# Grouped-query attention by single heads in another order, a convolution beside the projections, and a delta rule on four quadrants

## What is computed

```python
def odd_mixer(h, l, P, rope, ctx):
    z = jnp.dot(h, P['w_in_cd'][li])
    qkv, gate, beta_logit, decay_logit, qg, kg, vg = split_last(z, ...)
    y_c, delta_state = gated_delta_mixer(qkv, gate, ...)      # conv of 4 taps, silu, delta rule
    q = rms_norm(qg...); k = rms_norm(kg...)                   # 8 query heads, 2 key heads, width 64
    ...                                                        # rope; sample: 128 cached keys in front
    o = sweep_query_blocks(lambda qb: gqa_block(qb, k, v), q)  # softmax(q k) v
    return jnp.dot(concatenate([y_c, o]), P['w_out'][l])

def chunk_gated_delta_rule(q, k, v, beta, g, s0):              # chunks of 64 rows, forward and backward
    decay = jnp.exp(where(incl, G[..., :, None] - G[..., None, :], -inf))
    a = jnp.where(strict, einsum('nbhid,nbhjd->nbhij', kb, k) * decay, 0.0)
    sol = triangular_solve(a + eye(C), [kb * exp(G), v * beta])  # w, u
    ...                                                        # then a scan over the chunks carries the state
```

## Time and profile before

| | |
|---|---|
| three runs | 1832.85, 1833.32 and 1834.61 us, median 1833.32 |
| the profiled execution | 1830.64 us, span 1828.7 us |
| busy, share of the span | PE 1606.4 us (88%), DVE 647.2 (35%), ACT 449.8 (25%), POOL 195.5 (11%) |
| projections of layer 1, TensorE without a break | to 1057 us |
| attention, first to last pair's maximum | 1071.06 to 1158.69 us |
| convolved channels turned | 1164.95 to 1182 us |
| delta rule's levels | 1197 to 1363 us |

### The profile page before, as it was taken

One profiled execution on the slowest core, in us unless ns is written; L12 is line 12 of the kernel. 1 busy time (PEld: TensorE's weight loads), 2 busy tenths in 40 slices (PEclk: granted clock), 3 DMA queues, 4 the chain that ended last, 5 costly groups with the idle time before them and its releaser, 6 DMA issues.

```text
span 1828.7 us, 37469 instructions
## 1 busy us (share of the span) xinstructions
PE 1606.4 (88%) x16530; PEld 1036.2 (57%) x16530; DVE 647.2 (35%) x1284; ACT 449.8 (25%) x746; POOL 195.5 (11%) x197
## 2 busy tenths in 40 slices
PE   5999975778958999999999977899989959999992
PEld 2554433454525766764555455577775537767761
DVE  5234475553171000003135069844462171000003
ACT  4111184442031111112110045642231031111110
POOL 0000000000001111100000000055540001111113
PEclk8999987998989999999999999899999989999996
DMA  9922380457126999995121100000005126999994
GB/s 348 307 93 92 105 320 0 140 182 276 46 104 244 370 384 383 386 384 185 46 88 54 46 1 1 1 3 3 3 3 196 46 104 223 368 378 389 375 396 146
DMA packets 90316, 330.05 MB, mean 180 GB/s; under 512 B 10708, under 2 KB 16456, under 8 KB 82024
## 3 DMA queue, kind: packets, MB, share of 16 engines
q1 hardware_dynamic: 76016, 287.29, 41.3%
q0 software_dynamic: 9168, 32.65, 6.5%
q10 hardware_dynamic: 5032, 8.65, 1.3%
HBM read 303.79 MB, written 24.78 MB: 180 GB/s over the span
## 4 chain that ended last, share of the span: by engine, by line
PE 74%; DVE 12%; ACT 5%; DMA 4%; issue 4%; ACTq 0%; POOL 0%; DVEq 0%; SPq 0%
PE pairs L192 26%; PE pairs L1256 15%; PE pairs L1268 12%; PE pairs L1239 2%; DMA ring<-in_exp_w 2%; DVE sm L1615 1%; PE pairs L310 1%; PE pairs L1950 1%; PE pairs L1952 1%; PE pairs L971 1%; PE pairs L1683 1%; PE pairs L1939 1%; ACT arena L1531 1%; ACT arena L324 1%; PE pairs L426 1%
## 5 line engine op out<-in xcount | busy, mean ns | idle before, releaser
L192 PE MATMUL pairs<-hT,ring 128*128 128x128 f32 (+1 forms) x1120 | 305.6, 435 | 2.2 <-ACT hT L324 2.2
L192 PEld LDWEIGHTS pairs<-hT,ring 128*128 128x128 f32 x1120 | 170.0, 191 | 138.6 <-issue 136.2
L324 ACT ACTIVATE arena<-pairs 128x512 f32<-128x512 f32 (+7 forms) x212 | 129.3, 633 | 479.8 <-PE pairs L192 251.0
L192 PE MATMUL pairs<-ring,hT 128*128 128x512 f32 (+1 forms) x448 | 177.4, 557 | 0.0
L1256 PEld LDWEIGHTS pairs<-arena,ring 128*64 128x64 f32 x4096 | 143.0, 137 | 15.7 <-issue 15.6
L1256 PEld LDWEIGHTS pairs<-arena 128*64 128x64 f32 x4096 | 142.9, 137 | 14.2 <-issue 14.1
L1256 PE MATMUL pairs<-arena,ring 128*64 128x80 f32 x4096 | 146.1, 233 | 2.4 <-issue 2.4
L1256 PE MATMUL pairs<-arena 128*64 128x80 f32 x4096 | 145.8, 233 | 2.5 <-issue 1.4
L192 PEld LDWEIGHTS pairs<-ring,hT 128*128 128x128 f32 x448 | 84.8, 190 | 92.1 <-issue 89.1
L1324 DVE TENSOR_SCALAR hT<-pairs,arena 80x512 f32<-80x512 f32 x32 | 23.9, 747 | 272.8 <-ACT hT L1300 272.8
L1268 PE MATMUL pairs<-ring,arena 128*80 128x512 f32 x256 | 112.7, 593 | 0.8 <-DMA ring<-in_exp_w 0.8
(11 more groups left out here) (376 smaller groups left out, 2093.0 us busy)
## 6 DMA issues: line engine op xcount, KB each, us to landing
arena<-in_exp_w SPq DMA_DIRECT2D x48, 2048.0 KB, 19.0
ring<-in_exp_w SPq DMA_DIRECT2D x48, 2048.0 KB, 20.8
ring<-in_w_mod SPq DMA_DIRECT2D x24, 2048.0 KB, 8.2
ring<-in_w_in_ab SPq DMA_DIRECT2D x5, 2048.0 KB, 11.4
ring<-in_w_in_cd SPq DMA_DIRECT2D x5, 2048.0 KB, 9.0
ring<-in_w_out SPq DMA_DIRECT2D x4, 2048.0 KB, 9.1
moe_rows<-arena POOLq DMA_DIRECT2D x2, 2560.0 KB, 14.6
h_rows<-arena POOLq DMA_DIRECT2D x2, 2560.0 KB, 8.4
```

The source lines that it names most:

```text
L192: last = pe.matmul(out, lhs(k), rhs(k), start=(k == 0), stop=(k == KD - 1))
L324: return eng.activation(dst, src, ACT.Copy) if eng is nc.scalar else eng.tensor_copy(dst, src)
```

## The change

Attention, in TensorE's stream: the scores of one head are complete (512 and 128 columns) before those of the other, and each head has its own semaphores for maximum, reciprocal and scaling. The order becomes scores i, rows i-2, turn i-1. The scaling goes from VectorE to GpSimd (`gqa_pool`, new). Of the ten turned blocks ScalarE copies six and VectorE four (`rest`).

Convolution: the 16 taps of a chunk of channels stand behind VectorE's reads of that chunk (`delta_conv_dve`, new), all 12 SiLUs behind ScalarE's reads of chunk 2 (`delta_silu_act`, new). The scratch for the taps moves from hT, which the projections still read, to a free part of the arena.

Delta rule: `level_w` and the transposed part of `level_x` write the other half of the output's partitions, so the operands of X and XT lie in four different quarters of the array; `am` forms both the matrix and its transpose. X and XT have a bank each, 2e and 2e+1. For this the other units change banks: WU of even chunks stays in 6 and 7, that of odd ones goes to 4 and 5; vs goes from 4 to 6, o from 5 to 7, the state updates from 2 and 3 to 4 and 5, kT, kk and the decay sums from 6 to 1, qT from 7 to 3, qd from 7 to 6. `spare` waits for bank 7 and fills it.

```diff
+        def delta_conv_dve(v, c):
...
+                    y, x = cv[ct % 2], pad[:, ct, tap:tap + UW]
+                    if tap == 0:
+                        v.tensor_scalar(y, x, w, None, ALU.mult).then_inc(S("cv_tap"), 1)
+                    else:
+                        v.scalar_tensor_tensor(out=y if tap < 3 else pad[:, ct, 0:UW], in0=x, scalar=w, in1=y,
+                                               op0=ALU.mult, op1=ALU.add).then_inc(S("cv_tap"), 1)
...
+        def delta_silu_act(act):
+            for ct in range(12):
+                act.wait_ge(S("cv_tap"), 4 * ct + 4)
+                act.activation(pad[:, ct, 0:UW], pad[:, ct, 0:UW], ACT.Silu).then_inc(S("cv_silu"), 1)
...
-                    act.wait_ge(S("g_norm"), 2 * (j - 3))
-                for e in range(2):
-                    u = ("gs", j, e)
-                    release(act.activation(gp[j % 2][:, e, 0:n], filled(act, u)[:, 0:n], ACT.Exp, bias=nmax(j, e),
-                                           accum_out=psum_of(j, e)), u)
+                    act.wait_ge(S("g_recip"), 2 * (j - 4) + e + 1)
+                u = ("gs", j, e)
+                release(act.activation(gp[j % 2][:, e, 0:n], filled(act, u)[:, 0:n], ACT.Exp, bias=nmax(j, e),
+                                       accum_out=psum_of(j, e)), u)
...
+                u = ("gaT", j)
+                release(copy(act, gaT[j % 2][:, 0:n], filled(act, u)[:, 256:256 + n]), u)
+
+            for i in range(len(GP) + 2):
+                if 0 <= i - 2 < len(GP):
+                    turned(i - 2)
+                if i < len(GP):
+                    exps(i, 0)
...
+            def rest(j):
+                if GP[j][0] < ST:
+                    if j >= 2:
+                        v.wait_ge(S("g_result"), j - 1)
+                    v.wait_ge(S("g_rest"), j + 1)
+                    v.tensor_copy(gaT[j % 2][:, 768:1280], gupper[:, 0:512]).then_inc(S("g_rest_read"), 1)
+
+            def result(j):
+                t, m = GP[j]
+                v.wait_ge(S("g_result"), j + 1)
+                v.tensor_copy(hT[:, 4 + m, t * P:t * P + P], gupper[:, 512:640]).then_inc(S("g_result_read"), 1)
+
+            for i in range(len(GP) + 3):
+                if 0 <= i - 1 < len(GP):
+                    recip(i - 1, 0)
+                if 0 <= i - 2 < len(GP):
+                    rest(i - 2)
+                if 0 <= i - 3 < len(GP):
+                    result(i - 3)
+                if 0 <= i - 1 < len(GP):
+                    recip(i - 1, 1)
+                if i < len(GP):
+                    maxes(i, 0)
+                    maxes(i, 1)
+
+        def gqa_pool(g):
+            for j in range(len(GP)):
                 n = T if GP[j][0] < ST else P
...
+                    p = gp[j % 2][:, e, 0:n]
+                    g.tensor_tensor(p, p, rsum(j, e).broadcast_to((P, n)), ALU.mult).then_inc(S("g_norm"), 1)
...
+            def scores(j, e):
...
                 if t < ST:
-                    for e in range(2):
-                        pe.matmul(ps[e][:, 0:512], q[e], k[e][:, 0:512], start=True, stop=True)
-                    for e in range(2):
-                        finish(pe.matmul(ps[e][:, 512:T], q[e], k[e][:, 512:T], start=True, stop=True), ("gs", j, e))
+                    pe.matmul(ps[:, 0:512], q, k[:, 0:512], start=True, stop=True)
+                    finish(pe.matmul(ps[:, 512:T], q, k[:, 512:T], start=True, stop=True), u)
...
+            def turn(j, e):
+
...
-                for e in range(2):
-                    for b in range(nk):
-                        last = pe.transpose(gturn[:, (e * nk + b) * P:(e * nk + b + 1) * P],
-                                            gp[j % 2][:, e, b * P:b * P + P], ident)
-                finish(last, u)
+                ps = take(pe, u, 2) if e == 0 else PSUM[:, 2, :]
+                for b in range(nk):
+                    k = e * nk + b
+                    if k == 6 and j:
+                        pe.wait_ge(S("g_rest_read"), j)
+                    out = ps[:, 256 + P * k:384 + P * k] if k < 6 else gupper[:, P * (k - 6):P * (k - 5)]
...
+            for i in range(len(GP) + 2):
+                if i < len(GP):
+                    scores(i, 0)
+                    scores(i, 1)
+                if 0 <= i - 2 < len(GP):
+                    rows(i - 2)
+                if 0 <= i - 1 < len(GP):
+                    turn(i - 1, 0)
+                    turn(i - 1, 1)
...
+                for u, x, b in ((("kT", m), dk, 1), (("qT", m), dq, 3)):
                     ps = b_take(pe, u, b)
...
-                ps = b_take(pe, u, 6)
+                ps = b_take(pe, u, 1)
...
                 u = ("dec", j)
-                b_finish(dec_sums(pe, b_take(pe, u, 6), j), u)
+                b_finish(dec_sums(pe, b_take(pe, u, 1), j), u)
...
             def am(j):
                 pe.wait_ge(S(f"dl_am{j % 2}"), 6 * (j // 2) + 1)
-                u = ("am", j)
-                ps = b_take(pe, u, j % 2)
+                ut = ("amT", j)
+                if j >= 2:
+                    b_emptied(pe, ("w", j - 2, 5))
+                ps, pt = bank_of(2 * (j % 2)), b_take(pe, ut, 2 * (j % 2) + 1)
                 for h in range(4):
-                    for r in HALF:
-                        last = pe.matmul(ps[r, CK * h:CK * h + CK], am64(j)[r, h, :], C64["ident"][r, :],
+                    for r, other in (HALF, HALF[::-1]):
+                        pe.matmul(ps[other, CK * h:CK * h + CK], C64["ident"][r, :], am64(j)[r, h, :],
+                                  start=True, stop=True)
+                        last = pe.matmul(pt[r, CK * h:CK * h + CK], am64(j)[r, h, :], C64["ident"][r, :],
+                                         start=True, stop=True)
+                b_finish(last, ut)
...
+                for h in range(4):
+                    for r, other in (HALF, HALF[::-1]):
+                        last = pe.matmul(ps[other, CK * h:CK * h + CK], am64(j)[r, h, :], xt64(j)[r, h, :],
                                          start=True, stop=True)
                 b_finish(last, u)
...
             def level_x(j, s):
                 b_emptied(pe, ("w", j, s))
-                u = ("x", j, s)
-                ps = b_take(pe, u, j % 2)
+                ut = ("xT", j, s)
+                ps, pt = bank_of(2 * (j % 2)), b_take(pe, ut, 2 * (j % 2) + 1)
                 for h in range(4):
-                    for r in HALF:
+                    for r, other in (HALF, HALF[::-1]):
                         if s < 5:
                             pe.matmul(ps[r, CK * h:CK * h + CK], wt64(j)[r, h, :], x64(j)[r, h, :],
                                       start=True, stop=True)
-                        last = pe.matmul(ps[r, 256 + CK * h:256 + CK * h + CK], x64(j)[r, h, :], wt64(j)[r, h, :],
+                        last = pe.matmul(pt[other, CK * h:CK * h + CK], x64(j)[r, h, :], wt64(j)[r, h, :],
                                          start=True, stop=True)
-                b_finish(last, u)
+                b_finish(last, ut)
...
             def wu(j):
-                b_emptied(pe, ("x", j, 5))
+                b_emptied(pe, ("xT", j, 5))
                 pe.wait_ge(S("dl_vb"), j + 1)
                 pe.wait_ge(S(f"dl_kv{j % 2}"), j // 2 + 1)
                 us = [("wu", j, b) for b in range(2)]
-                ps = [b_take(pe, us[b], 6 + b) for b in range(2)]
...
             def spare():
-                if banks.uses[4]:
-                    pe.wait_ge(bank_free[4], banks.uses[4])
-                keep_busy(pe, bank_of(4), 1)
+                if banks.uses[7]:
+                    pe.wait_ge(bank_free[7], banks.uses[7])
+                keep_busy(pe, bank_of(7), 1)
```

More of the change, by code:

```diff
@@ L1673, in gqa_pe @@
             emptied(pe, ("gkT", 1))
-            def scores(j):
+            def scores(j, e):
                 t, m = GP[j]
-                ps = [take(pe, ("gs", j, e), e) for e in range(2)]
-                q = [gqT[64 * e:64 * e + 64, m, t * P:t * P + P] for e in range(2)]
-                k = [gkT[64 * e:64 * e + 64, m // 2, :] for e in range(2)]
+                u = ("gs", j, e)
+                ps = take(pe, u, e)
+                r = slice(64 * e, 64 * e + 64)
+                q, k = gqT[r, m, t * P:t * P + P], gkT[r, m // 2, :]
@@ L2065, in delta_pe @@
             state_b(9)
-            pe.wait_ge(bank_free[4], banks.uses[4])
-            keep_busy(pe, bank_of(4), 6)
+            pe.wait_ge(bank_free[6], banks.uses[6])
+            keep_busy(pe, bank_of(6), 6)
             pe.wait_ge(S("o_done"), 10)
@@ L2108, in delta_act @@
             act.activation(heads5(qsq), heads4(dq), ACT.Square).then_inc(S("qk_sq"), 1)
-            for ct in range(8, 12):
-                silu(ct)
             for c in range(4, 8):
```

190 lines of the change are left out of this document (80 added, 110 removed).

## The result

The changed kernel takes 1811.24 us (median of 4 runs, 1810.07 to 1812.83), the kernel before 1833.09 us in the same comparison (4 runs); the ratio is 0.9885, 95% interval [0.9866, 0.9904]. 1811 was forecast. The profiled execution took 1811.86 us, its span is 1809.9.

What follows compares the result with a forecast made beforehand. VectorE was taken to bound attention and TensorE the delta rule. Terms -14.9 - 3.2 - 1.5 - 2.7 = -22.3 us took the profiled 1830.6 to 1808.3, for a median of 1811 us; own range 1802 to 1819, 8-in-10 range 1800 to 1825.

Steps and rivals of the forecast that it cites:

- Projections: Layer 1 projections: the moved taps and SiLUs fit beside TensorE's work there and cost nothing.
- Attention, -14.9: Sixteen large pairs of heads: each falls from 4.83 to 3.90 us with TensorE the bound, 14.9 us gained.
- VectorE is the bound: Grouped-query attention before the change: VectorE, 18.36 us of 20 busy, was taken as what bounds it.
- Small pairs and join, -3.2 - 1.5 = -4.7: Four small pairs gain 3.2 us without taps; the passage from attention into the delta rule gains 1.5 us.
- Delta rule, -2.7: Delta rule: gains from four array quadrants, less new waits on shared banks and fillers, sum to -2.7 us.
- rival 2: Delta rule gets slower by its shared banks, +8 us, total 1821.7 us; chance 0.20.
- the sum's bounds: Delta rule: -14 us if all 20 levels gain and only fillers lose, +8 if quadrants bring nothing.
- fillers: Delta rule, between the two WU products: filler waits for bank 7, 0.95 us lost, five times, +4.75 us.
- Rival 1: Attention: score products run serially, 4.6 us per pair, total 1822.2 us; chance 0.12.
- rival 3: Attention: TensorE's clock stays at 1.2 GHz, about 6.9 us per pair, total 1859 us; chance 0.04.
- rival 4: End of kernel: experts' weights come at their own time, so the total stays within 0.2%; chance 0.03.
- signs of being wrong: Score products not overlapping; GpSimd at 1.8 us or more, or TensorE awaiting it; longer delta-rule steps; half clock through attention.

Runs made afterwards that it cites:

- e1: Kernel before with only the convolution's taps and SiLUs moved beside the projections; 1827.42 us, ratio 0.9962.
- e4: The changed kernel run once more, unaltered; 1813.42 us, ratio 0.9891 to the kernel before.
- e9: Changed kernel with the scaling of attention's probabilities on VectorE again instead of GpSimd; 1810.10 us, ratio 0.9908.
- e3: Changed kernel's convolution and attention, with the delta rule and all banks of the kernel before; 1809.17 us, ratio 0.9877.
- e10: Changed kernel with TensorE's old order in attention, transposes ahead of the value products; 1813.38 us, ratio 0.9907.
- e8: Changed kernel with both heads' 512-column score products side by side again, then both of 128; 1819.28 us, ratio 0.9931.
- e2: Changed kernel with the taps back in attention, about two per pair, and the SiLUs behind attention; 1825.40 us, ratio 0.9950.
- e7: Changed kernel with the edits of both e5 and e6; 1794.70 us, ratio 0.9795.
- e11: Kernel of e7 with one more filler product in each of the four small pairs of attention; 1793.89 us, ratio 0.9801.
- e12: Kernel of e7 with a filler product ahead of each of the eight decay sums; 1796.15 us, ratio 0.9808.
- e5: Changed kernel with decay sums, key transposes and key products in bank 6, query transposes in bank 7; 1803.40 us, ratio 0.9845.
- e6: Changed kernel with the filler of the delta rule's steps in bank 4 instead of 7; 1808.04 us, ratio 0.9871.

## Why the prediction was right, and where it was not

The forecast 1811 and the measured 1811.24 agree better than the terms behind them.

- **Projections.** Right. 48 taps stand beside them (VectorE 19.1 us busy of 20 at 980 to 1000), and the first scores come at 1070.7, within the scatter.
- **Attention, -14.9.** The sixteen large pairs: 3.89 us instead of 3.90 in the steady state; from the first to the last scores 74.2 to 58.4 us, -15.8. Right, and for the right reason in the new kernel: its scores overlap, and TensorE is the bound, with the second head's bank free just too late in every second pair, as the working said (3.9 us against 3.78).
- **"VectorE is the bound" before.** Wrong, though no term hung on it. I took the busiest engine for the bound. The rows said otherwise: in the earlier trace rows TensorE waits for ScalarE's exponentials, and in the earlier trace rows the maximum itself waits 0.29 us for the scores. e1 shows it: without the taps the pair stays at 4.83. The bound was the ring of a joint maximum, which starts only when both heads are done, and frees no bank until both exponentials are through. Had only the taps been moved, my sentence would have forecast 12 us too much.
- **Small pairs and join, -3.2 - 1.5 = -4.7.** Measured from the last large scores to the first channel transpose: 21.2 to 16.3 us, -4.9. The transposes themselves ran at the full clock in this profile and gave 1.6 more; in e4 they took 17.3 us and gave nothing.
- **Delta rule, -2.7.** Measured +4.9, so rival 2 had the sign; the sum's bounds held it. The failing step is the sum of its terms, in two ways. First its waits and gains, here laid beside each other piece by piece from the timelines, where the clock is full before and after:

| us | forecast | measured |
|---|---|---|
| levels 1 and 3, steps 1 to 3: X and XT 1.91 to 0.98 | -5.4 | -5.6 |
| two key tiles in step 0 | +1.6 | +1.3 |
| levels 2 and 4, steps 0 to 3: decay sums to the end of XT, 3.12 to 3.28 | 0 | +1.3 |
| third key tile, in step 2: its transposes to the next `am`, 3.1 to 4.9 | not counted | +1.7 |
| levels 1 to 4 of the last step: first X to first WU product, 20.8 to 18.8 | -3.6 | -1.9 |
| fillers: second WU product 0.96 later (3.43 to 4.39 after the first), 0.4 of it back in the piece behind four of them | +4.75 | about +3.8 |
| first `am` to first key transposes, 4.2 to 3.2 | 0 | -1.0 |

  The eight waits for the decay sums are as forecast (8.5 us, 8 x 1.1). What failed are the third key tile, the last step and levels 2 and 4, 4.7 us together, of which the last two rows give 2 back: the sum is -0.4 and not -2.7, and the stage as a whole is +0.1 at equal clock (e9). Second the clock, to which the sum gave no term: the other 4.7 us. These nine profiles have the old or the changed code in that stage:

| delta rule | us | at 1.2 GHz |
|---|---|---|
| as before (before, e1, e3) | 187.1, 187.0, 187.2 | 6.8 each |
| changed, e9 | 187.3 | 6.8 |
| changed, e10 | 188.9 | 13.7 |
| changed, e8 | 192.1 | 17.1 |
| changed, after | 192.0 | 20.5 |
| changed, e4 | 193.5 | 23.9 |
| changed, e2 | 195.0 | 27.3 |

  At the same 6.8 us the changed stage is as long as the old one (+0.1 to +0.3), by the one profile that there is (e9): the quadrants give just what the shared banks take. Each us more at 1.2 GHz costs about 0.38 us ((195.0 - 187.3) / (27.3 - 6.8); 0.23 to 0.47 for the four profiles between), and the changed stage had 18 us of it on average over its six profiles, against 6.8 in each of the three of the old one. Two of the three stretches after, and the one of before:

```profile
1310.00:1318.00 8.00, 6.49 (x112) 5.41 (x114) 5.41 (x11) 1.35 (x4) 3.19 (x4) 0.58 0.01 2
1352.00:1363.00 11.00, 9.74 (x78) 7.38 (x76) 2.25 (x4) 2.86 (x6) 0.00 (x0) 0.53 0.00 0
```

```profile
1338.00:1346.00 8.00, 7.50 (x64) 5.27 (x59) 3.00 (x6) 0.95 (x2) 4.17 (x5) 0.57 0.02 4
```

  Ahead of the first of them TensorE had worked little, 1.42 us of 4:

```profile
1308.00:1312.00 4.00, 1.42 (x8) 0.68 (x4) 3.16 (x6) 1.91 (x4) 4.00 (x5) 0.90 0.01 2
```

  If waits let the clock fall, they cost a second time. The runs suggest it (17.2 us of new waits and 7 to 27 us at 1.2 GHz; 0 to 10 us in e7, e11 and e12, which have none of them), but e9 has all these waits and only 6.8 us, and e5 and e6 have fewer and 17 and 24 us. So it stays open what decides whether the clock falls at a place.
- **Sum.** Attention and what follows gave 22.3 us and not 19.6, the delta rule took 4.9 and did not give 2.7, and the unedited stages scattered by -1.5: 22.3 - 4.9 + 1.5 = 18.9, the difference of the spans being 18.8. The medians differ by 21.9. So the exact hit is partly luck; the range of 1800 to 1825 was earned. (The chances of forecast and rivals 1 and 2 add up to 0.93, not 0.92.)
- **Rival 1** (serial scores) is refuted by the trace and by e8; **rival 3** did not occur, the clock is 1.00 in the profile from 1080 us on to the last large pair; **rival 4** neither, every us of attention arrives. Of the signs of being wrong one came, a delta rule longer than before.
- On the order of products: after the change, too, the second head's wide product starts ahead of the first head's narrow one (1094.27 and 1095.24 above). The rule of the Trainium skill (TensorE: Matmul & The Clock Gate, "Part 3: Packing small matmuls") that products keep program order would, by the prediction's working, have made the pair 4.6 us; the trace disagrees, with 3.89.

## What to carry to other kernels

A busy engine is not the bound; ask what each wait ends on. An engine at 92% stood beside a ring of dependent steps, and relieving it gave the large pairs nothing while the ring was whole (4.83 us in e1). With the ring cut in two the same relief was worth 0.2 us per pair (4.1 in e2, 3.89 in the changed kernel). When products are spread over more quarters of the array, give them banks of their own: here the same quarters are worth nothing at equal clock with the banks shared, and 14 us without that (e7). Equal code had 7 to 27 us at the lower clock here, and whether waits bring that on stayed open, so compare stages at equal clock before a cause is named.

## What was not expected of the hardware

- The delta rule took 187.3 to 195.0 us in six profiles of kernels with equal code there, with 6.8 to 27.3 us at 1.2 GHz. The clock at one place depends on more than the code at that place.
- VectorE's maximum over 640 columns takes 0.82 us, over 2 x 640 in one instruction 1.49: two instructions next to each other take 1.55, so they cost 0.06 us more than one.
- GpSimd's multiplication by a factor per row takes 0.40 us for 128 columns and 1.25 for 640; with the 1.04 for 512 that is 1.67 ns per further column. The prediction's line of 1.2 ns went through a 256-wide row with two full operands; it came near (1.20 us) because 640 is close to 512.

```profile
L1672 POOL TENSOR_TENSOR arena<-arena,sm 128x640 f32<-128x640 f32 x32 | 40.0, 1252 | 85.9 <-DVE sm L1639 85.9
...
L1672 POOL TENSOR_TENSOR arena<-arena,sm 128x128 f32<-128x128 f32 x8 | 3.2, 399 | 4.6 <-DVE sm L1639 4.6
```
